# First W1 panels gated ahead of the modulation tiles, and gate vectors transposed on VectorE and stored by rows, in a two-model transformer kernel

## What is computed

```python
def ffn_sublayer(h, m, sub, g_pre, g_post, w1, w2):
    shift, scale, gate = mods_of(m, sub)
    y = swiglu(modulate(rms_norm(h, g_pre[sub]), shift, scale), w1, w2)
    return h + MACARON_WEIGHT * gate * rms_norm(y, g_post[sub])

def swiglu(h, w1, w2):
    gate, up = jnp.split(h @ w1, 2, axis=-1)
    return (jax.nn.silu(gate) * up) @ w2
...
for layer in range(DEPTH):
    mod = (c_act @ w_mod[layer] + b_mod[layer]).reshape(b, 1, N_MOD, D_MODEL)
    mod_c = (cc_act @ w_mod[layer] + b_mod[layer]).reshape(N_MOD, D_MODEL)
```

## Time and profile before

| what | value |
|---|---|
| median of 3 runs | 2794.22 us (2792.9 to 2795.83) |
| profiled execution, time | 2796.88 us |
| profiled execution, span | 2795.1 us |
| TensorE matmul busy | 2660.0 us (95%) |
| VectorE busy | 1321.9 us (47%) |
| ScalarE busy | 647.9 us (23%) |
| GpSimd busy | 1345.4 us (48%) |
| mean granted TensorE clock | 0.986 of full |

### The profile page before, as it was taken

One profiled execution on the slowest core, in us unless ns is written; L12 is line 12 of the kernel. 1 busy time (PEld: TensorE's weight loads), 2 busy tenths in 40 slices (PEclk: granted clock), 3 DMA queues, 4 the chain that ended last, 5 costly groups with the idle time before them and its releaser, 6 DMA issues.

```text
span 2795.1 us, 42372 instructions
## 1 busy us (share of the span) xinstructions
PE 2660.0 (95%) x16880; PEld 2252.6 (81%) x16880; DVE 1321.9 (47%) x2098; ACT 647.9 (23%) x1191; POOL 1345.4 (48%) x608
## 2 busy tenths in 40 slices
PE   9999999999999979998999999999999999897998
PEld 7988787699878857887888688888888888775996
DVE  1762843267275436674241633444355443534237
ACT  3432212254221220001131731001230011425001
POOL 4830100375010015665645636666556556667886
PEclk9999999999999989999999999999999999999999
DMA  6543412454442246666223035442355543322444
GB/s 232 194 167 119 167 61 92 158 181 165 150 166 77 77 139 242 230 231 91 105 78 118 16 85 209 166 165 90 105 198 193 193 107 108 119 91 76 146 170 150
DMA packets 81316, 393.24 MB, mean 141 GB/s; under 512 B 31648, under 2 KB 33184, under 8 KB 34848
## 3 DMA queue, kind: packets, MB, share of 16 engines
q1 hardware_dynamic: 57424, 311.92, 32.5%
q10 hardware_dynamic: 23760, 79.44, 8.7%
HBM read 390.23 MB, written 1.10 MB: 140 GB/s over the span
## 4 chain that ended last, share of the span: by engine, by line
issue 25%; POOL 11%; POOLq 10%; PE 9%; DMA 5%; SPq 1%; DVE 1%; ACT 0%; DVEq 0%; ACTq 0%
POOL m_ws L1697 9%; POOLq L1696 7%; DMA m_ring<-in_panels 5%; PE m_bank L1854 2%; POOLq L1709 2%; POOL m_ws L1715 1%; SPq L1653 1%; PE m_bank L1780 1%; PE m_bank L1781 1%; PE m_bank L1782 1%; POOLq L1714 1%; PE m_bank L1987 1%; PE m_bank L1999 1%; PE m_bank L2014 1%; PE m_bank L1950 1%
## 5 line engine op out<-in xcount | busy, mean ns | idle before, releaser
L1780 PE MATMUL m_bank<-m_aT,m_ws 128*128 128x512 f32 (+1 forms) x1792 | 632.6, 353 | 40.0 <-DVE m_aT_low L2402 15.9
L1781 PE MATMUL m_bank<-m_aT_low,m_ws 128*128 128x512 f32 (+1 forms) x1792 | 628.7, 351 | 0.0
L1782 PE MATMUL m_bank<-m_aT,m_ws 128*128 128x512 f32 (+1 forms) x1792 | 628.6, 351 | 0.0
L1697 POOL TENSOR_TENSOR m_ws<-m_ring,m_ws 128x2048 fp32r<-128x2048 f32 x127 | 593.9, 4677 | 18.7
L1854 PE MATMUL m_bank<-m_ws,m_hs 128*128 128x512 f32 x1848 | 424.8, 391 | 11.6 <-POOL m_ws L1697 7.6
L1854 PEld LDWEIGHTS m_bank<-m_ws,m_hs 128*128 128x128 f32 x1848 | 347.1, 188 | 88.6 <-issue 16.1
L1780 PEld LDWEIGHTS m_bank<-m_aT,m_ws 128*128 128x128 f32 x1792 | 345.7, 193 | 88.0 <-issue 31.0
L1781 PEld LDWEIGHTS m_bank<-m_aT_low,m_ws 128*128 128x128 f32 x1792 | 345.9, 193 | 42.5
L1782 PEld LDWEIGHTS m_bank<-m_aT,m_ws 128*128 128x128 f32 x1792 | 345.4, 193 | 42.7
L350 POOL TENSOR_TENSOR m_ws<-m_ring,m_ws 128x2048 fp32r<-128x2048 f32 x48 | 221.2, 4628 | 321.8 <-ACT m_ws L859 321.8
L1708 POOL TENSOR_TENSOR m_small<-m_small 128x1 f32<-128x1 f32 x158 | 32.6, 206 | 561.8 <-PE m_bank L1782 375.8
(11 more groups left out here) (352 smaller groups left out, 3625.0 us busy)
## 6 DMA issues: line engine op xcount, KB each, us to landing
m_ring<-in_panels SPq DMA_DIRECT2D x286, 1024.0 KB, 4.8
m_y<-in_w_mod_t ACTq DMA_DIRECT2D x43, 1024.0 KB, 4.9
m_prob<-in_w_mod_t ACTq DMA_DIRECT2D x21, 1024.0 KB, 4.9
m_rows<-m_gg_dram ACTq DMA_DIRECT2D x6, 1024.0 KB, 4.7
m_bias<-in_rpb SPq DMA_DIRECT2D x48, 64.0 KB, 2.6
m_rows<-in_c_rows ACTq DMA_DIRECT2D x3, 1024.0 KB, 4.7
m_ring<-in_panels SPq DMA_DIRECT2D x4, 512.0 KB, 5.1
m_hT<-in_ln_rows ACTq DMA_DIRECT2D x2, 1024.0 KB, 6.5
```

The costliest lines, as they stand in the source:

```text
L1697: nc.gpsimd.tensor_tensor(ws[:, p, 1, :], ring[:, p, :], ws[:, p, 0, :].bitcast(F32), ALU.subtract)\
L1780: mm(out, w, a, start=start, stop=False)
L1781: mm(out, w, a_low, start=False, stop=False)
L1782: return mm(out, w_low, a, start=False, stop=stop)
```

## The change

In feed-forwards e = 0, 2 and 3, on both ScalarE and VectorE, the first two W1 panels are handled before the silu of the conditioning rows and before the first modulation tile. `mod_done` spreads the tiles over the 19 panels 1 to 19 instead of the 20 panels 0 to 19. The gate vectors are transposed on VectorE in 32x32 blocks into `gg_t` and each sublayer's gate is stored with four transfers of 16 rows of 32 elements instead of one transfer of single elements. `gg` is zeroed once at the start of the second model. In e = 2 and 3 VectorE waits, ahead of the transpose, for the earlier stores.

```diff
@@
+        gg_t = sb("gg_t", [P, DEPTH * 6 * KD])
...
         def mod_done(e, q):
-            return MOD_AT[e] + len(MOD_TILES[e]) * (q + 1) // (FF - 2)
+            return MOD_AT[e] + len(MOD_TILES[e]) * q // (FF - 3)
@@ store_gates
-                    act.dma_start(gg_dram[3 * l + sub, :].rearrange("(s k p) -> p s k", s=2, p=P), gg[:, 3 * l + sub, :, :],
-                                  allow_slow_non_contiguous=True).then_inc(s["gg_st"], 16)
-                    gate_stores[0] += 1
+                    j = 3 * l + sub
+                    for b in range(4):
+                        r0 = 32 * b + 16 * (j % 2)
+                        act.dma_start(gg_dram[j, :].rearrange("(c b q) -> b c q", b=4, q=32)[b],
+                                      gg_t[r0:r0 + 16, 32 * (j // 2):32 * (j // 2) + 32]).then_inc(s["gg_st"], 16)
+                        gate_stores[0] += 1
@@ ScalarE, feed_forward
-                    act.wait_ge(s["aT_split"], KD * (IN_STREAMS[e] + 2))
-                    act.wait_ge(s["rows_in"], 16 * (row_loads(e) - 1))
-                    for v in range(2):
-                        last = a_(c_row[v], rows[:, v, :], ACT.Silu)
-                    last.then_inc(s["c_row_in"], 1)
                     for q in range(FF - 2):
                         swish(q % 2, q // 2)
+                        if q == 1:
+                            act.wait_ge(s["aT_split"], KD * (IN_STREAMS[e] + 2))
+                            act.wait_ge(s["rows_in"], 16 * (row_loads(e) - 1))
+                            for v in range(2):
+                                last = a_(c_row[v], rows[:, v, :], ACT.Silu)
+                            last.then_inc(s["c_row_in"], 1)
@@ VectorE, start
             scales(0, 0)
+            V.memset(gg[:, :, :, :], 0.0)
             dve.drain()
@@ VectorE, feed_forward
-                    dve.wait_ge(s["c_row_in"], list(MOD_TILES).index(e) + 1)
-                    mod_products(e, MOD_AT[e], mod_done(e, 0))
                     for q in range(FF - 2):
                         gated(q % 2, q // 2)
+                        if q == 1:
+                            dve.wait_ge(s["c_row_in"], list(MOD_TILES).index(e) + 1)
                         if q:
                             mod_products(e, mod_done(e, q - 1), mod_done(e, q))
...
                     if e == 0:
                         gates(0, 0)
+                    else:
+                        dve.wait_ge(s["gg_st"], 64 * (3 if e == 2 else 4))
+                    dve.drain()
+                    for b in ((0, 1), (), (1,), (2,))[e]:
+                        V.transpose(gg_t[:, 32 * b:32 * b + 32], gg[:, 2 * b:2 * b + 2, :, :].rearrange("p e s k -> p (e s k)"))
                     dve.drain()
```

## The result

| | median, us | runs | ratio to before, 95% interval |
|---|---|---|---|
| before | 2795.83 | 7 | |
| after | 2781.99 | 7 | 0.9938 (0.9924 to 0.9952) |

The change makes the kernel faster by 13.8 us between the medians. The ratio was estimated apart from the medians, whose quotient is 0.9950; it stands for 17.3 us (13.4 to 21.2), and 13.8 us lies inside its interval. The forecast was 7.75 us. The profiled execution took 2783.06 us, its span 2781.3 against 2795.1 us, and TensorE's matmuls were busy for 2658.2 us against 2660.0.

The account below looks back on a forecast made before the run. TensorE bounds the kernel, busy 2660.0 of 2795.1 us. Gains at panel 2 of 4.92 + 1.97 (e = 0), 0 (e = 2) and 0.86 (e = 3) sum to 7.75 us: median 2786.5 us, range 2783.5 to 2791.5.

Parts of the forecast that it names:

- The chain of waits at panel 2: e = 0, panel 2 of W1: rows' load, silu, tile, gated unit, TensorE; TensorE stands still 6.39 us.
- the floor of 1.5 us by GpSimd's split: Panel 2: a gap of about 1.5 us remains when TensorE waits for GpSimd's split alone.
- The full clock behind it: e = 0, behind panel 2's shortened gap: ten matmuls run at full clock instead of 0.50, gaining 1.97 us.
- The costs put at nothing: Two-tile slots, transposes (0.5 us, 2.2 us cover), stores' issues (4.6 to 14.2 us) and memset: each cost 0.
- the clock rival: e = 0: clock stays low after the gap of 1.46 us; gain 5.8 us, 2788.4 us; chance 0.12.
- the one of the transposes: Last slot, e = 0 and 3: transposes come behind GpSimd's next low half; 13.5 us slower, 2807.7 us; chance 0.06.
- the fourth rival: e = 0: something else holds the first swish until after 1057.6; half the gain, 2790.5 us; chance 0.07.
- handed back: Rival: panel 2's gain is lost again in the loop through overrun slots; 2793 to 2795 us; chance 0.12.
- three signs of being wrong: Gap at W2's start, granted clock 0.50 behind the short gap, or e = 0's gap longer than 2 us.
- the sentence on the stores: W2: faster landing gains nothing, first read-back comes 95 us later, GpSimd waits for TensorE; cost 0, gain 0.
- The sentence behind it: Stores: 2048 descriptors against 64 by the skill's rule, yet the same sum, as no one waits for either.
- The term of e = 0: Panel 2 of e = 0: restart 4.92 us earlier, plus 1.97 us from the full clock.

Follow-up runs that it names:

- stores alone: Kernel before with only the new gate stores (transposes, memset, rows of 32 elements), old order of panels and tiles: 2788.16 us, ratio 0.9959.
- order alone: Kernel before with only the new order of panels and tiles, gates stored in the old single-element form: 2794.01 us, ratio 0.9983.
- each store twice: Kernel before with each old gate store issued twice, copies to rows nobody reads: 2822.32 us, one run.
- one old store: Kernel before with one of e = 0's three old stores left in W2, the two others issued in e = 1: 2790.27 us, ratio 0.9965.
- 64-byte runs: Kernel before with each gate stored as 128 pieces of 64 bytes, so gates are read back in another order: 2789.13 us, ratio 0.9965.
- two old stores: Kernel before with two of e = 0's three old stores left in W2, the third issued in e = 1: 2791.74 us, ratio 0.9974.

## Why the prediction was wrong

**What was right.** The chain of waits at panel 2, and the floor of 1.5 us by GpSimd's split: 1.36, 1.46 and 1.48 us. The full clock behind it. Place by place: 5.03 us less of a gap in e = 0 against 4.92, 0.87 against 0.86 in e = 3, none in e = 2. The costs put at nothing held as well: two transposes took 0.30 us together, by VectorE's timeline of the changed kernel, the wait behind GpSimd is what it was the earlier trace rows, and W2 starts without a gap.

```profile
1268.48 4.68 DVE L2338 SCALAR_TENSOR_TENSOR m_gg<-mod,m_vec 128x16 f32<-128x16 f32 x2
1273.23 0.30 DVE L2480 STREAM_TRANSPOSE m_gg_t<-m_gg 128x32 f32<-128x32 f32 x2
```

The twelve issues took 6.17 us (ScalarE's timeline of the changed kernel), inside the 4.6 to 14.2 of the prediction, and the refill behind them kept no one waiting.

```profile
1278.29 6.17 ACTq L2150 DMA_DIRECT2D m_gg_dram<-m_gg_t  x12
```

Neither the clock rival nor the one of the transposes came, the first swish began at 1051.92 and not behind the floor (the fourth rival), and the balance above (11.31 us against terms of 11.40) leaves nothing handed back in e = 0. None of the three signs of being wrong that the prediction named appeared either. They were all drawn from the places that it had looked at, so they couldn't catch a gain elsewhere.

**The step that failed** is the sentence on the stores: "No GpSimd wait for a ring load falls there either, since it waits for TensorE. Cost 0, gain 0." The row it cites, at 1282.58, is of the first gate in W2, which indeed waits for TensorE. The wait for the ring is two gates later, at 1315.46. One row was taken for the whole of W2. The landing of the stores (12.6 to 28.0 us) said which window to search, and the prediction used it only to ask who reads the stores. The sentence behind it, that rule and row give the same sum "as no one waits for either", asked for waits on the transfer and not for those on what shares its engines. What the runs showed in its place: the stores hold up a ring load to 25.5 us, GpSimd waits 14.73 us for it and TensorE 7.60 us for GpSimd. The terms left out are 7.60 us and 1.83 us of clock, 9.4 us in all; the stores alone measured 11.5 (8.1 to 15.1).

**A size that was off.** The term of e = 0 (4.92 + 1.97 us) is no constant of the kernel before. The order alone gave 4.8 us (2.5 to 7.3) where 7.75 were forecast. In every kernel with the old order TensorE's gap at panel 2 is the time from the issue of the conditioning rows' load to the table load that follows its landing, less a fixed 1.81 us:

| kernel (old order) | rows' load issued to table load, us | gap, us | difference | second ring load issued ahead of it by, us | lost by the clock behind the gap, us |
|---|---|---|---|---|---|
| before | 1045.30 to 1053.49: 8.19 | 6.39 | 1.80 | 4.7 | 2.2 |
| each store twice | 1045.51 to 1053.66: 8.15 | 6.34 | 1.81 | 4.6 | 2.7 |
| one old store | 1046.86 to 1054.58: 7.72 | 5.90 | 1.82 | 4.8 | 2.4 |
| stores alone | 1046.91 to 1052.26: 5.35 | 3.54 | 1.81 | 5.6 | 1.7 |
| 64-byte runs | 1050.10 to 1055.04: 4.94 | 3.13 | 1.81 | 6.0 | 2.9 |
| two old stores | 1050.80 to 1055.70: 4.90 | 3.09 | 1.81 | 5.6 | 0.0 |

The last column is half of the time at the granted clock 0.50, from stretches of 0.25 us; for the kernel before the prediction had 1.97 us by counting matmuls. None of these edits touches what runs ahead of panel 2, apart from a memset in one, so the load's time varies from run to run. The fifth column shows what it goes with: SP issues two ring loads of 1024 KB, 0.6 us apart, just ahead of the rows' load. Where the second went 4.6 to 4.8 us ahead, it landed 6.1 to 6.4 us behind the issue of the rows' load, and the rows took 7.4 to 7.8 us. Where it went 5.6 to 6.0 us ahead, it landed 2.0 to 2.1 us behind that issue, and the rows took 4.6 to 5.0 us. So the two loads meet more or less, and no experiment set their distance on purpose. The timelines of ScalarE and TensorE with the stores alone:

```profile
1046.91 0.33 ACTq L2180 DMA_DIRECT2D m_rows<-in_c_rows  x1
...
1052.26 1.28 ACT L2187 ACT_TABLE_LOAD   x1 [4.75 <-DMA m_rows<-in_c_rows]
...
1061.32 0.47 PE L1781 MATMUL m_bank<-m_aT,m_ws 128*128 128x512 f32 x1 [3.54 <-DVE m_hidT L2450]
```

Its clock behind that gap, with the columns of the stretches above:

```profile
1061.30:1062.50 1.20, 1.18 (x5) 1.03 (x6) 1.07 (x2) 0.00 (x0) 1.05 (x2) 1.00 0.89 375
1062.70:1066.00 3.30, 3.30 (x10) 2.56 (x9) 3.30 (x7) 0.00 (x0) 3.30 (x1) 0.50 0.98 397
```

The profile shown before the prediction had the slowest load of the six. The new order takes this load off the path: the gap is 1.36 us, at full clock, in the three profiles with the new order and whole panels. By the two ends of the table the restart is worth 1.7 to 5.0 us, and the clock 0 to 2.9 more. As an estimate from the means of the six rows, the order is worth 4.73 - 1.36 = 3.4 us of gap, 2.0 us of clock and 0.9 us in e = 3, so 6.2 us, which lies inside the 2.5 to 7.3 that were measured; 7.75 lies above them.

Put together: the order's 4.8 us and the stores' 11.5 us are 16.3, and the whole change measured 17.3 (13.4 to 21.2). The forecast was thus too large by some 3 us where it looked and lacked 9 to 12 us where it didn't.

## What to carry to other kernels

Before a transfer is costed at nothing, list every load that is issued while it is in flight, on any queue, and read their landings: a store of 8 KB in 4-byte pieces delays a neighbour, though nobody waits for the store itself. Read the whole table of waits for the stretch, also the groups that the change doesn't name: the row of 10.6 us stood next to the one of 10.2 us that the prediction used. A gap that ends with a load's landing varies with that load, so take its size from more than one execution, and look at what else was in flight.

## What the runs showed of the hardware

- A store of 2048 separate elements of 4 bytes (8 KB) added 5.8, 8.5 and 6.4 us (the first, second and third at a time) to the landing of a load of 1024 KB on another queue, whose own time is 4.8 us. In pieces of 64 bytes (128 of them) the same 8 KB landed in 1.4 to 1.5 us, and its four transfers in pieces of 128 bytes in 1.3 to 4.0 us each; both delayed nothing that could be seen.
- An issue of such a store behind others took up to 15.85 us on ScalarE's queue, and with six in a row the engine did nothing else for 38.35 us. With three it was 0.38 to 1.18 us each.
- Two loads of 1024 KB on two queues that were issued within 0.1 us of each other took 7.7 to 8.1 us each (three profiles); a ring load issued 0.3 to 0.4 us ahead of the other took 4.8 to 5.1 us (seven profiles).
- The first matmul behind a gap doesn't tell the clock of the stretch. Behind a TensorE gap of 3.54 us it took 0.47 us (the full clock), but the granted clock fell to 0.50 some 1.4 us later and stayed there for 3.4 us. Behind the gap of 2.22 us in the last W2 of the changed kernel it was 1.00 for about 1 us and then 0.50 for 3.3 us. Behind 3.13 us it was 0.50 at once, for 5.7 us, and behind 3.09 us it stayed at 1.00. The gaps of 5.90 to 20.15 us in the tables and rows above were all followed by 0.50 at once, those of 1.30 to 1.48 us and the one of 2.35 us by 1.00. From 2.2 to 3.6 us the length of the gap alone doesn't tell what follows.
